# A hybrid decoder step: the RMS norm's token scale moved from the block's input to its outputs

## The reference, cut to what matters

```python
def rms_norm(x, g):
    y = xf * lax.rsqrt(jnp.mean(xf * xf, axis=-1, keepdims=True) + EPS)
    return (y * g)

def swiglu(h, w_up, w_down):
    g, u = jnp.split(h @ w_up, 2, axis=-1)
    return (jax.nn.silu(g) * u) @ w_down

for l in range(DEPTH):
    if l == N_A_LAYERS:
        k_new, v_new = shared_kv(x, g_kv, w_kv, g_k_b)      # rms_norm(x, g_kv) @ w_kv
    x = x + 0.5 * swiglu(rms_norm(x, g_ffn1[l]), w_ffn1_up[l], w_ffn1_down[l])
    h = rms_norm(x, g_mix[l])
    mix = mixer(h @ w_in, ...)                              # gates, convolution, heads, memory
    x = x + mix @ w_out[l]
    x = x + 0.5 * swiglu(rms_norm(x, g_ffn2[l]), w_ffn2_up[l], w_ffn2_down[l])
```

## Time and profile before

| | |
|---|---|
| Runs, us | 2866.9, 2875.16, 2872.56 (median 2872.56) |
| Span of the profiled execution, first to last instruction | 2854.5 |
| What lies around the span in the three runs | 12.4 to 20.7 |
| TensorE, VectorE, ScalarE busy in the span | 94%, 38%, 31% |
| Mean granted TensorE clock | 0.944 of full |
| Matmuls | 18953 |

### The profile page before, as it was taken

One profiled execution on the slowest core, in us unless ns is written; L12 is line 12 of the kernel. 1 busy time (PEld: TensorE's weight loads), 2 busy tenths in 40 slices (PEclk: granted clock), 3 DMA queues, 4 the chain that ended last, 5 costly groups with the idle time before them and its releaser, 6 DMA issues.

```text
span 2854.5 us, 44327 instructions
## 1 busy us (share of the span) xinstructions
PE 2686.6 (94%) x18953; PEld 2545.1 (89%) x18953; DVE 1089.9 (38%) x1361; ACT 872.7 (31%) x1025; POOL 93.6 (3%) x178
## 2 busy tenths in 40 slices
PE   7999998999886999999989999999978799999999
PEld 6999998999655889999989999999954588999998
DVE  7333234651444243323354323224238414333223
ACT  5332222542123233212232332223344322332221
POOL 1000000000112000000000000001000110000000
PEclk8999999999798899999989999999888868999999
DMA  5323322122222122232223222323210222323322
GB/s 165 92 77 87 86 66 62 56 86 66 54 86 63 45 74 74 80 96 73 67 70 120 80 74 81 89 72 115 79 39 33 71 76 60 89 66 92 84 66 79
DMA packets 334514, 220.61 MB, mean 77 GB/s; under 512 B 11849, under 2 KB 326497, under 8 KB 334420
## 3 DMA queue, kind: packets, MB, share of 16 engines
q1 hardware_dynamic: 325268, 185.83, 22.6%
q0 software_dynamic: 9152, 33.43, 3.7%
HBM read 206.78 MB, written 12.45 MB: 77 GB/s over the span
## 4 chain that ended last, share of the span: by engine, by line
PE 90%; DVE 6%; ACT 2%; issue 1%; DMA 0%; SPq 0%; POOL 0%; DVEq 0%; ACTq 0%
PE psum L505 68%; PE psum L523 6%; PE psum L2120 1%; PE psum L2141 1%; PE psum L1364 1%; DVE tmp L765 1%; PE psum L1423 1%; PE psum L1415 1%; PE psum L1674 1%; PE psum L1970 1%; DVE rest L2043 1%; DVE act_lo L759 1%; PE psum L1554 1%; PE psum L2142 1%; PE psum L1959 1%
## 5 line engine op out<-in xcount | busy, mean ns | idle before, releaser
L505 PE MATMUL psum<-act_hi,whi 128*128 128x288 f32 (+2 forms) x3504 | 754.6, 297 | 21.4 <-DVE act_lo L759 15.3
L505 PE MATMUL psum<-act_lo,whi 128*128 128x288 f32 (+2 forms) x3504 | 753.1, 297 | 0.0
L505 PE MATMUL psum<-act_hi,wlo 128*128 128x288 f32 (+2 forms) x3504 | 752.7, 297 | 0.0
L505 PEld LDWEIGHTS psum<-act_hi,whi 128*128 128x128 f32 (+2 forms) x3504 | 563.3, 188 | 25.3 <-issue 13.9
L505 PEld LDWEIGHTS psum<-act_hi,wlo 128*128 128x128 f32 (+2 forms) x3504 | 563.9, 188 | 0.5
L505 PEld LDWEIGHTS psum<-act_lo,whi 128*128 128x128 f32 (+2 forms) x3504 | 563.8, 188 | 0.5
L484 DVE TENSOR_TENSOR wlo<-raw,whi 128x2048 fp32r<-128x2048 f32 x190 | 435.4, 2292 | 297.6 <-ACT whi L477 297.5
L477 ACT ACTIVATE whi<-raw 128x2048 fp32r<-128x2048 f32 x190 | 362.4, 1907 | 272.2 <-PE psum L505 271.8
L505 PE MATMUL psum<-h_lo,whi 128*128 128x288 f32 x1408 | 302.1, 295 | 0.0
L505 PE MATMUL psum<-h_hi,wlo 128*128 128x288 f32 x1408 | 301.9, 295 | 0.0
L505 PE MATMUL psum<-h_hi,whi 128*128 128x288 f32 x1408 | 301.9, 295 | 0.0
(11 more groups left out here) (389 smaller groups left out, 2316.2 us busy)
## 6 DMA issues: line engine op xcount, KB each, us to landing
raw<-in_w_ffn_up SPq DMA_DIRECT2D x176, 512.0 KB, 4.9
raw<-in_w_ffn_down SPq DMA_DIRECT2D x64, 384.0 KB, 4.0
raw<-in_w_ffn_down SPq DMA_DIRECT2D x64, 320.0 KB, 3.6
raw<-in_w_out SPq DMA_DIRECT2D x16, 512.0 KB, 4.4
raw<-in_w_in_a SPq DMA_DIRECT2D x14, 512.0 KB, 4.7
raw<-in_w_in_a SPq DMA_DIRECT2D x16, 384.0 KB, 3.9
raw<-in_w_kv SPq DMA_DIRECT2D x12, 512.0 KB, 4.1
vpg<-in_cache_v POOLq DMA_DIRECT2D x16, 384.0 KB, 3.6
```

What stands on the lines that cost most here:

```text
L505: last = pe.matmul(psum[0:width, 4 * j + 2 * m + h, 0:HALF], w[:, k, cols], a[:, k, h * HALF:(h + 1) * HALF], start=(k == 0 and step == 0) ...
```

## The change

The scale per token is no longer multiplied into x. Only the gain is (`gained_hi` on ScalarE, `gained_lo` on VectorE, from x_t directly, without tmp), and that happens as soon as a chunk of x is final: in the last down tiles of an FFN, behind the last OUT tile, behind the last K/V tile. The chain of sums, root and spread is issued inside the next block's first weight tile: in a product tile the sums behind chunk 3 and the spread behind chunk 5, in a natural tile behind token tiles 1 and 2. The scale, kept in rinv by a VectorE copy, is applied where results leave PSUM: two VectorE products per FFN up tile, then the silu on ScalarE from SBUF and one more VectorE product; six VectorE products per head tile in place of four ScalarE copies; in natural tiles as ScalarE's per-partition scale, one op per token tile. In INA a natural tile (the output gate's first) now goes first and the gates' tile second, and the turns of the convolution's history stand behind the gates' tile. The K/V norm's and FFN2's inputs share one scale as before.

```diff
@@ product / natural_product
+                if norm is not None and k == 3:
+                    norm_sums_pe(pe, norm)
+                if norm is not None and k == 5:
+                    norm_spread_pe(pe, norm)
...
+                if norm is not None and t == 1:
+                    norm_sums_pe(pe, norm)
+                if norm is not None and t == 2:
+                    norm_spread_pe(pe, norm)
@@ the norm
+        def norm_sums_pe(pe, g):
             pe.wait_ge(S.sum_done, 9 * g + 9)
-            if g:
-                pe.wait_ge(S.region_free1, n_next // 2)
-            for t in range(TT):
-                at = t * P if t < 4 else TOK - P
-                last = pe.matmul(norm_cols(g)[:, t:t + 1], sumsq[:, at:at + P], ones[:, 0:1], start=True, stop=True)
+            for t in range(4):
+                pe.matmul(norm_cols()[:, t:t + 1], sumsq[:, t * P:(t + 1) * P], ones[:, 0:1], start=True, stop=True)
+            for r in (0, NSA):
+                last = pe.matmul(norm_cols()[r:r + NSA, 4:5], sumsq[:, NPR:TOK], ones[:, 0:1], start=True, stop=True)
             last.then_inc(S.sumsq_ready, 1)
...
+        def norm_dve(dve, g):
+            dve.wait_ge(S.rms_ready, g + 1)
+            dve.reciprocal(rcols[:, :], rcols[:, :]).then_inc(S.rinv_cols, 1)
+            dve.wait_ge(S.rinv_spread, g + 1)
+            dve.tensor_copy(rinv[:, :], flat[:, RINV_AT:RINV_AT + TOK]).then_inc(S.rinv_kept, 1)
+            dve.wait_ge(S.rinv_kept, g + 1)
+
+        def gained_hi(act, k, gains):
+
+            act.activation(act_hi[:, k, :], x_t[:, k, :], ACT.Copy, scale=gains[:, k:k + 1]).then_inc(S.nh_ready, 1)
+
+        def gained_lo(dve, k, gains, nth):
+            dve.wait_ge(S.nh_ready, 8 * nth + k + 1)
+            dve.scalar_tensor_tensor(act_lo[:, k, :], x_t[:, k, :], gains[:, k:k + 1], act_hi[:, k, :].bitcast(F32),
+                                     ALU.mult, ALU.subtract).then_inc(S.nl_ready, 1)
@@ ffn_act, up tiles
                         split_hi(act, n + 1, 1 - j)
-                        act.wait_ge(S.tile_done, n + 1)
-                        act.activation(halves(sg[j][:, :]), region(j)[:, 0:2, 0:HALF], ACT.Silu).then_inc(S.sg_ready, 1)
-                        act.wait_ge(region_free[j], n_up // 2 + i + 1)
+                        if norm is not None and j == 0:
+                            norm_act(act, norm)
+                        act.wait_ge(S.gate_scaled, 2 * i + (ups + j + 1))
+                        act.activation(sg[j][:, :], sg[j][:, :], ACT.Silu).then_inc(S.sg_ready, 1)
+                        act.wait_ge(S.h_mixed, 2 * i + (ups + j + 1))
@@ ffn_dve, up tiles
+                        dve.wait_ge(S.tile_done, n + 1)
+                        dve.tensor_tensor(halves(sg[j][:, :]), region(j)[:, 0:2, 0:HALF], halves(rinv[:, :]), ALU.mult) \
+                            .then_inc(S.gate_scaled, 1)
+                        dve.tensor_tensor(halves(h_raw[j][:, :]), region(j)[:, 2:4, 0:HALF], halves(rinv[:, :]), ALU.mult) \
+                            .then_inc(region_free[j], 1)
+                        dve.wait_ge(region_free[j], n_up // 2 + i + 1)
                         dve.wait_ge(S.sg_ready, 2 * i + (ups + j + 1))
-                        dve.tensor_tensor(halves(h_raw[j][:, :]), halves(sg[j][:, :]), region(j)[:, 2:4, 0:HALF], ALU.mult) \
-                            .then_inc(region_free[j], 1)
+                        dve.tensor_tensor(h_raw[j][:, :], sg[j][:, :], h_raw[j][:, :], ALU.mult).then_inc(S.h_mixed, 1)
@@ ffn down tiles of the second part: ffn_act, then ffn_dve
+                            gained_hi(act, 2 * i + j, gains)
                             square(act, j, 2 * i + j, g, 2 * i + j)
...
+                            gained_lo(dve, 2 * i + j, gains, nth)
                             sum_square(dve, j, g, 2 * i + j)
@@ out_act, then out_dve
+                if t == 3:
+                    act.wait_ge(S.tile_done, n + 1)
+                    gained_hi(act, 0, gains)
+                    gained_hi(act, 1, gains)
...
                 for m in range(2):
+                    if t == 3:
+                        gained_lo(dve, m, gains, nth)
                     x = halves(x_t[:, 2 * t + m, :])
@@ ina_dve, head tiles
+                    for m in range(2):
+                        dve.tensor_tensor(cb[j][:, m, 3:3 + HALF], src[:, m, 0, :], rinv[0:DH, 0:HALF], ALU.mult)
+                        dve.tensor_tensor(cb[j][:, m, 3 + HALF:3 + NPR], src[:, m, 1, 0:NPR - HALF], rinv[0:DH, HALF:NPR], ALU.mult)
+                        ins = dve.tensor_tensor(cb_sample(j, m)[:, :, 3:3 + NS], seg(src[:, m, 1, NPR - HALF:HALF]),
+                                                seg(rinv[0:DH, NPR:TOK]), ALU.mult)
+                    ins.then_inc(region_free[j], 1)
@@ kv_act
-                act.activation(dst[:, 0:4, cols_], src[:, 0:4, :], ACT.Copy)
-                act.activation(dst[0:NSA, 4, cols_], src[0:NSA, 4, :], ACT.Copy).then_inc(region_free[j], 1)
+                for i, _, rows in token_tiles():
+                    ins = act.activation(dst[0:rows, i, cols_], src[0:rows, i, :], ACT.Copy, scale=rcols[0:rows, i:i + 1])
+                ins.then_inc(region_free[j], 1)
@@ kv_dve, behind the K/V tiles
                 dve.tensor_copy(kt_b[:, k, :], flat[:, 1024 * (k % 3):1024 * (k % 3) + TOK]).then_inc(S.kt_copied, 1)
+                if k in (2, 3, 4):
+                    gained_lo(dve, k - 2, gains, nth)
@@ vector program, ahead of the first out_dve
+            dve.wait_ge(S.head_stored, 48 * HA)
@@ tensor program (the same at the other norms)
-            norm_pe(pe, 2, BASE_FFN[1])
-            ffn_pe(pe, 1, 2)
+            ffn_pe(pe, 1, 2, 2)
```

More of the change, by code:

```diff
@@ L492, in start_tile, with product @@
                 pe.wait_ge(region_free[j], (n - j) // 2)
-        def product(pe, n, j, w_hi, w_lo, a_hi, a_lo, chunks, outs, width, ready=None):
+        def product(pe, n, j, w_hi, w_lo, a_hi, a_lo, chunks, outs, width, ready=None, norm=None):
             start_tile(pe, n, j)
@@ L727, in norm_pe @@
                 n = P if t < 4 else NSA
[L728 to L729 removed]
+                last = pe.matmul(flat[:, RINV_AT + t * P:RINV_AT + t * P + n], rcols[:, t:t + 1].broadcast_to([P, P]),
+                                 ident[:, 0:n], start=True, stop=True)
             last.then_inc(S.rinv_spread, 1)
[L732 to L741 removed]
@@ L812, in mem_act @@
                 act.activation(small[:, 0:8], small[:, 0:8], ACT.Sqrt, scale=1.0 / DM, bias=eps[:, :]).then_inc(S.mk_rms, 1)
-            norm_act(act, 0, 0, False, between=lambda: split_hi(act, 4, 0))
+            norm_act(act, 0)
+            split_hi(act, 4, 0)
+            for k in range(KD):
+                gained_hi(act, k, gain("ffn1", 0))
         def mem_dve(dve, c):
@@ L844, in mem_dve @@
             values(0)
-            norm_dve(dve, 0, 0, False, gain("ffn1", 0), between=lambda: split_lo(dve, 4, 0))
+            norm_dve(dve, 0)
+            split_lo(dve, 4, 0)
+            for k in range(KD):
+                gained_lo(dve, k, gain("ffn1", 0), 0)
             values(1)
@@ L907, in ffn_act, with up @@
                     act.wait_ge(*((S.keys_stored, 32), (S.kv_stored, 64))[q // 2])
-                with act.Fori(0, chunks // 2) as i:
+                def up(i, norm=None):
                     for j in range(2):
@@ L922, in down @@
                             act.wait_ge(region_free[j], n_down // 2 + i + 1)
+                            gained_hi(act, 2 * i + j, gains)
                             square(act, j, 2 * i + j, g, 2 * i + j)
-                if n_down + KD == N_TILES:
+                if part and g is not None:
+                    for i in range(KD // 2):
+                        down(i)
+                elif n_down + KD == N_TILES:
                     with act.Fori(0, KD // 2 - 1) as i:
@@ L935, in ffn_dve, with up @@
                     dve.wait_ge(*((S.keys_stored, 32), (S.kv_stored, 64))[q // 2])
-                with dve.Fori(0, chunks // 2) as i:
+                def up(i, norm=None):
                     for j in range(2):
@@ L945, in ffn_dve @@
                                           ALU.subtract).then_inc(S.hl_ready, 1)
+                if part == 0:
+                    up(0, norm)
+                with dve.Fori(1 if part == 0 else 0, chunks // 2) as i:
+                    up(i)
                 if part and g is not None:
@@ L1000, in out_dve @@
                     sum_square(dve, m, g, 2 * t + m)
+                    if t == 3:
+                        gained_lo(dve, 2 + m, gains, nth)
+            for k in range(4, KD):
+                gained_lo(dve, k, gains, nth)
         def end_pe(pe):
@@ L1864, in kv_pe, with kv_act @@
             pe.wait_ge(S.kt_copied, 6)
-        def kv_act(act):
+        def kv_act(act, norm, gains):
             for t in range(6):
@@ L1882, in kv_act, with kv_dve @@
                     act.activation(small[:, 40:60], small[:, 40:60], ACT.Sqrt, scale=1.0 / DB, bias=eps[:, :]).then_inc(S.k_rms, 1)
```

(4 more changed lines are left out.)

333 lines of the change are left out of this document (164 added, 169 removed).

## The result

Before took 2872.02 us in the median, after 2802.02: the ratio is 0.9769, with a 95% interval of 0.9747 to 0.9791. That is 70.0 less; the forecast was 60.8 less, at 2812. In a later comparison it was 2869.95 against 2805.58: 0.9789 (0.9761 to 0.9816), 64.4 less. The forecast's 60.8 lies inside both intervals. The range of 2800 to 2834 holds both medians, near its low end. Over all timed executions on record the mean is 2868.6 for the kernel before (49 executions on several chips) and 2805.2 for the kernel after (nine), which is 63.4 less.

What follows compares the result with a forecast made beforehand. TensorE, with 90% of the chain of waits, bounds the kernel. Gains and losses by block sum to 60.8 us: span 2854.5 becomes 2793.7, plus 18.1 gives 2811.8, forecast 2812, range 2800 to 2834.

Steps and rivals of the forecast that it cites:

- The input block: First input block, from FFN0's end to the second head's start: 38.9 us, a gain of 17.9.
- the second head's wait: Input block: the second head waits 1.3 us for the gates' chain and the history copy behind it.
- FFN1 and FFN3: Blocks after an output projection: gains of 8.2 and 8.8 us, with TensorE starting 1.7 after the last matmul.
- the stall: FFN1 and FFN3: TensorE waits 1.35 us at chunk 2 for VectorE's copies.
- norm work: Sums and spread moved into the first tile: 2.5 us of TensorE time per norm, 5.2 at the gap's pace.
- just in time: FFN1 and FFN3: reciprocal done at 13.9 us, TensorE asks for the spread at 13.95; late-root rival, chance 0.08.
- granted clock 1.00 through the first tiles: Sign that the forecast holds: full clock in first tiles; rival of a falling clock there: 9 us, 2821, chance 0.14.
- K/V and query block: Gains of 16.6 and 9.2 us, with no gap before the first matmul.
- FFN2: The gap behind the key transposes stays; 24.00 us becomes 24.3, a gain of -0.3.
- Up tiles at no cost: 88 FFN up tiles: 1.5 us more VectorE work each, cost 0; rival that VectorE's chain overruns the tile: chance 0.05.
- The setup's 1.1: Setup: ScalarE's copies no longer wait for scaled ones, so the wait for the second tile's split goes: gain 1.1 us.
- 18.1 above the span of the profiled execution; that part is outside the blocks and stays: Whole program: 18.1 us between span and three-run median, added to the predicted span of 2793.7 to give 2811.8.

Runs made afterwards that it cites:

- before's second and third profiles: The kernel before, unchanged, profiled twice more: 2872.26 us in the median with a profiled span of 2871.4, then 2862.71 with a span of 2861.1.
- Experiment 6: The kernel after with six more VectorE products of 128x576 in each up tile: 2816.85 us; in a second kernel six scans instead: 2872.61 us.
- after's second profile: The kernel after, unchanged, timed and profiled once more: 2805.58 us in the median, span 2801.2.

## Why the prediction came out as it did

- *The input block* was right to a tenth: 38.90 for the forecast's 38.9. Its parts balanced: the emptying of the natural tile began with a table load of 1.28 that was not counted and pushed the split to 508.68, and the second head's wait was 1.7, not 1.3. The emptying of a head took 1.66, not 1.9, and head tiles 89.45 / 7 = 12.78.
- *FFN1 and FFN3*: 8.3 and 7.7 for 8.2 and 8.8 (4.5 and 8.8 against before's first profile, the one that the forecast started from and whose quick loop in FFN1 hid 3.8). The start was 1.92 (1.7), the stall 0.79 in FFN3 and none in FFN1 (1.35), norm work 2.4 (2.5). The root was not just in time but 0.8 early. The clock fell in FFN1 all the same, which costs 1.7; "granted clock 1.00 through the first tiles" failed there.
- *K/V and query block*: 17.2 and 9.6 for 16.6 and 9.2, no wait and full clock, as said.
- *FFN2*: a loss of 0.7 for 0.3. Its gap and its lower clock stayed.
- *Up tiles at no cost*: right as far as waits go: TensorE has none inside after's up tiles, and FFN0 takes 422.2 in before's second and third profiles and in after's. Experiment 6 puts the edge between 4.1 and 8.1 more per tile. Open is the pace of 12.48, which only before's profiles have.
- *The setup's 1.1* was a term of that one execution, as its wait is absent in before's second and third profiles. Its mechanism holds where it applies: in after's second profile TensorE began FFN0's first tile at 59.8, earlier still, and did not wait behind it.
- *The step that failed* is the last of the sum: "18.1 above the span of the profiled execution; that part is outside the blocks and stays". Only 1.6 to 1.8 lie outside. The 16 were inside: the profiled execution had up tiles at 12.48 in two loops (some 6) and an attention at 299.4 (10.6 less than in the next two). That this did no harm is arithmetic and not insight: the 18.1 was worked out as the median less the span and then added to the span again, so it cancels, and the forecast is the median less 60.8. Its reason was wrong, and so was that for the range, whose 6 to 8 for the runs' spread has to cover these draws.
- *Luck*: that 60.8 lies so near 59.9 rests in part on errors that offset each other. In FFN1 the stall of 1.35 that didn't come made room for the clock's 1.7; in the input block the second head's wait was 0.4 longer and the tiles ahead of it ended 0.3 earlier than said.
- *What stays open*: 70.0 or 64.4 were measured and 63.4 by the means over all executions, 59.9 is shown in the rewritten stages. The attention's and mLSTM's times go with the clock granted in them. They range over 6 to 10 between kernels that share that code, yet after's attention drew 302.6 and 302.8 in its two profiles. Whether an earlier start of the attention brings a better clock there was not tried.

## What to carry to other kernels

A norm's scalar per token can leave the input path in full. Of some 60 us gained, taking the hidden chain away alone cost 36 (five places), and taking the early copies away alone 18 (three places), and the two overlap. The price was VectorE time that had cover. Before counting on cover, count the chain from the end of a tile to the last thing that the next but one needs, not the engine's busy share: VectorE had 57% of idle time, and 8 us more per 12.8 us tile ate the whole gain. And profile the kernel before at least twice: one execution's distance from the median is not a constant part of the program, and two copies of one program differed by 6 in the median.
